# Summing over partitions with the values stationary: the sample attention's last reduction in a hybrid decoder layer

## The reference, cut to what matters

```
for window, d in DILATED_PATTERNS:              # (128,1), (512,4), (2048,16)
    s = einsum('bshe,bsnhe->bhsn', qf, kg) * scale + bias
    p = exp(s - m); den = sum(p)
    o = einsum('bhsn,bsnhe->bshe', p, vg) / den
return combine_patterns(outs, lses)             # weighted by the denominators
...
a.reshape(B, T, D_ATTN) * silu(ga)              # gate of the attention branch
```

## Time and profile before

| | |
|---|---|
| median of 3 executions | 902.86 us (902.83 to 903.67) |
| the profiled execution | 903.18 us |
| its span in the trace | 901.3 us |
| TensorE (PE) busy | 859.9 us, 95% |
| VectorE (DVE) busy | 565.9 us, 63% |
| ScalarE (ACT) busy | 402.5 us, 45% |
| GpSimd (POOL) busy | 52.1 us, 6% |
| instructions | 17338 |

### The profile page before, as it was taken

The page is one execution under the profiler, slowest core; times in us unless marked ns, Lnnn a source line. Parts: engine busy times, 40 slices in busy tenths (PEclk is TensorE's granted clock), DMA queues, the critical chain, the costliest instruction groups (busy, mean ns, idle before and its releaser), DMA issues. The chain is left out here.

```text
span 901.3 us, 17338 instructions
## 1 busy us (share of the span) xinstructions
PE 859.9 (95%) x7014; PEld 847.0 (94%) x7014; DVE 565.9 (63%) x1035; ACT 402.5 (45%) x896; POOL 52.1 (6%) x96
## 2 busy tenths in 40 slices
PE   7999999999999999999999999999989999999991
PEld 7999999999999999999999999999978999999990
DVE  5546866668676768667786767687779633333332
ACT  5745335524543453355246434533555433444333
POOL 3000000001000000100010000000000000000000
PEclk9999999999999999999999999999999999999996
DMA  8363455364526635553554266355565434434324
GB/s 300 113 166 99 122 149 146 93 161 133 142 83 149 174 91 134 140 148 93 141 158 129 86 155 174 87 131 150 150 167 155 127 107 120 124 109 124 110 59 189
DMA packets 207048, 121.36 MB, mean 135 GB/s; under 512 B 7576, under 2 KB 201760, under 8 KB 206432
## 3 DMA queue, kind: packets, MB, share of 16 engines
q1 hardware_dynamic: 202520, 111.20, 44.7%
q0 software_dynamic: 4448, 9.05, 3.1%
HBM read 108.04 MB, written 12.63 MB: 134 GB/s over the span
## 5 line engine op out<-in xcount | busy, mean ns | idle before, releaser
L547 PE MATMUL pj<-mov_hi,w_hi 128*128 128x260 f32 x2048 | 423.0, 288 | 0.5 <-DVE mov_lo L1425 0.5
L547 PE MATMUL pj<-mov_hi,w_lo 128*128 128x260 f32 x2048 | 412.0, 283 | 0.0
L547 PE MATMUL pj<-mov_lo,w_hi 128*128 128x260 f32 x2048 | 411.4, 282 | 0.0
L547 PEld LDWEIGHTS pj<-mov_hi,w_hi 128*128 128x128 f32 x2048 | 315.3, 189 | 2.1 <-DVE mov_lo L1425 0.7
L547 PEld LDWEIGHTS pj<-mov_lo,w_hi 128*128 128x128 f32 x2048 | 315.8, 188 | 0.0
L547 PEld LDWEIGHTS pj<-mov_hi,w_lo 128*128 128x128 f32 x2048 | 315.4, 188 | 0.0
L1103 DVE TENSOR_TENSOR w_lo<-w_raw,w_hi 128x640 fp32r<-128x640 f32 (+1 forms) x192 | 166.3, 866 | 213.5 <-ACT w_hi L745 212.6
L745 ACT ACTIVATE w_hi<-w_raw 128x640 fp32r<-128x640 f32 (+1 forms) x192 | 147.6, 769 | 187.2 <-PE pj L547 183.5
L801 ACT ACTIVATE pt_hi<-ps_t 128x128 fp32r<-128x128 f32 (+1 forms) x64 | 26.2, 436 | 78.9 <-PE ps_t L555 72.2
L1186 DVE TENSOR_TENSOR pt_lo<-ps_t,pt_hi 128x128 fp32r<-128x128 f32 (+1 forms) x64 | 29.6, 484 | 43.0 <-ACT pt_hi L801 43.0
L785 ACT ACTIVATE arena<-arena,stat 128x128 f32<-128x128 f32 (+1 forms) x64 | 35.5, 555 | 35.8 <-DVE stat L1172 35.8
(11 more groups left out here) (161 smaller groups left out, 710.3 us busy)
## 6 DMA issues: line engine op xcount, KB each, us to landing
w_raw<-in_w_in SPq DMA_DIRECT2D x96, 320.0 KB, 3.3
w_raw<-in_w_in SPq DMA_DIRECT2D x48, 384.0 KB, 3.6
arena<-in_cache_k_win SPq DMA_DIRECT2D x16, 384.0 KB, 5.4
arena<-in_cache_v_win SPq DMA_DIRECT2D x16, 384.0 KB, 8.1
w_raw<-in_w_out SPq DMA_DIRECT2D x16, 384.0 KB, 3.7
w_raw<-in_w_out SPq DMA_DIRECT2D x16, 320.0 KB, 3.0
arena<-row_scratch POOLq DMA_DIRECT2D x8, 512.0 KB, 5.0
arena<-in_cache_k_win SPq DMA_DIRECT2D x8, 512.0 KB, 6.4
```

The costliest lines, as they stand in the source:

```text
L547: mm = pe.matmul(pj[a][h][:, 0:HT], w, m[:, k, HT * h:HT * h + HT], start=(k == 0 and i == 0), stop=(c == 2 and k == KT - 1 and i == 2))
```

## The change

The operands of the sum over partitions change places. For each of the 8 samples the 128 x 128 block of `av_hi`, and then that of `av_lo`, is stationary, and two columns of ones are moving: 16 matmuls with 16 weight loads in place of four and four. The result for sample `b` lands as a column (and a copy of it beside it) in `ps_m`, one channel on each partition, so nothing is left to pick: one VectorE instruction multiplies every other column of the first 16 with the gate and writes `attn`. `ps_t` and `o_side` are no longer used, the semaphore `pick` goes, and its waiters wait for `mixed` or for `pool_mixed`.

```
-                elif pr > 0:
-                    pe.wait_ge(pick, 4 * pr)
+                elif pr >= 2 and pr % 2 == 0:
+                    pe.wait_ge(pool_mixed, pr)          # turn_p
...
                     if pr > 0:
-                        pe.wait_ge(pick, 4 * pr)
+                        pe.wait_ge(mixed, pr)           # step 10
...
-                    for b, dst in ((0, ps_m), (1, ps_t)):
-                        cols = slice(512 * b, 512 * b + 512)
-                        pe.matmul(dst[:, :], ones_r[:, :], av_hi[:, cols], start=True, stop=False)
-                        pe.matmul(dst[:, :], ones_r[:, :], av_lo[:, cols], start=False,
-                                  stop=True).then_inc(av_sum, 1)
+                    for b in range(NB):
+                        cols, to = slice(P * b, P * b + P), ps_m[:, 2 * b:2 * b + 2]
+                        pe.matmul(to, av_hi[:, cols], ones_r[:, 0:2], start=True, stop=False)
+                        mm = pe.matmul(to, av_lo[:, cols], ones_r[:, 0:2], start=False, stop=True)
+                    mm.then_inc(av_sum, 1)
...
-                    pe.wait_ge(pick, 4 * PAIRS)
+                    pe.wait_ge(mixed, PAIRS)            # turn_y(0)
...
-                if h == 0 and pr > 0:
-                    act.wait_ge(pick, 4 * pr)           # side
...
             def pick_rows(pr):
-                for b, src in ((0, ps_m), (1, ps_t)):
-                    dve.wait_ge(av_sum, 2 * pr + b + 1)
-                    if b == 1:
-                        dve.wait_ge(pick, 4 * pr + 2)
-                    else:
-                        dve.wait_ge(o_done, 2 * pr + 2)
-                    tmp = o_side.rearrange("p (b e) -> p b e", b=4)
-                    dve.tensor_tensor(tmp, src[:, :].rearrange("p (b e) -> p b e", b=4),
-                                      ident.unsqueeze(1).to_broadcast([P, 4, P]),
-                                      ALU.mult).then_inc(pick, 1)
-                    dve.wait_ge(pick, 4 * pr + 2 * b + 1)
-                    dve.tensor_reduce(attn[:, SEQ + 4 * b:SEQ + 4 * b + 4], tmp, AX_X,
-                                      ALU.add).then_inc(pick, 1)
-                dve.wait_ge(pick, 4 * pr + 4)
+                dve.wait_ge(av_sum, pr + 1)
                 dve.wait_ge(ga_gate, pr + 1)
-                dve.tensor_tensor(attn[:, SEQ:NT], attn[:, SEQ:NT], z_ga[:, SEQ:NT],
+                dve.tensor_tensor(attn[:, SEQ:NT], ps_m[:, 0:2 * NB:2], z_ga[:, SEQ:NT],
                                   ALU.mult).then_inc(mixed, 1)
```

More of the change, by code:

```diff
@@ L319, in layer_step @@
         av_sum = sem("av_sum")
-        pick = sem("pick")
         attn_gated, mixed = sem("attn_gated"), sem("mixed")
```

## The result

| | before | after |
|---|---|---|
| median of five executions | 903.06 us (902.83 to 904.52) | 913.2 us (911.25 to 914.98) |
| the profiled execution, its span | 903.18 us, 901.3 us | 914.98 us, 912.8 us |
| ratio of the times, 95% interval | | 1.0105 (1.009 to 1.0121) |

The kernel is slower by 10.1 us. The forecast of slower was right, the size was not: 909.2 us with a range up to 911.5. The profiled execution is the slowest of the five, so its account has to come out at more than the median's.

What follows compares the result with a forecast made beforehand. TensorE, busy 859.9 of 901.3 us, was taken to bound the kernel. Eight sums at 0.80 us, 6.4, less 0.13 made 6.3 us more: 909.2 us median, 907 to 911 at 0.75, 80% range 905.8 to 911.5.

Steps and rivals of the forecast that it cites:

- the sum 6.4 - 0.13: Whole kernel: 6.4 us added by eight sums' weight loads, less 0.13 us for a wait at block 15, giving 6.3 us.
- rival 3: Clock falls behind each pair's tiny matmuls, counted as a stand: 13.6 us more, 923; chance 0.03.
- The shift per sum: At each of eight sums, TensorE's next job starts 0.80 us later, 6.4 us in all.
- My formula: Delay of TensorE's next job behind each sum: 16 t - 0.96 us, t being the distance of two weight loads.
- the load and not the matmul sets the distance: At the scores behind a sum: weight loads take 0.11 us, 128-column matmuls 0.07 or less, so 16 loads take 1.76 us.
- the bounds of t: Distance of two weight loads in the sum: between 0.07 and 0.18 us, 1.3 to 15.4 us in all; 0.11 taken.
- VectorE is paced by TensorE: Throughout: VectorE waits on ScalarE, which waits for TensorE, so the delay reaches the end and 22 us less work buys idle time.
- rival 2: VectorE sets TensorE's pace and its relief shortens TensorE's waits: up to 8.4 us won, 900.8 us; chance 0.03.
- VectorE would wait some 1.4 us for the sum: At each pair's small instruction: VectorE waits some 1.4 us at no cost, done by 135.7 to 136.2, before 137.34.
- the wait at block 15: First output tile: TensorE's wait for the low part of block 15 goes, since `mixed` comes sooner: -0.13 us.
- in one place alone: In the steps following the sum's VectorE work, VectorE was said to idle 1.89 us at a single place.
- the shorter waits that the prediction had named as a sign against it: TensorE's waits for the bias and `av_lo` should keep 7.6 and 3.2 us; shrinking waits would show the prediction wrong.

Runs made afterwards that it cites:

- e5: The changed kernel with 128 columns of ones moving under the same 16 loads in place of two, results in two banks: 909.96 us, ratio 1.0074.
- e2: The changed kernel with 64 columns of ones moving under the same 16 loads in place of two: 911.15 us, ratio 1.0088.
- e10: The changed kernel run once more, unchanged, for a second profile: 912.65 us, ratio 1.0108 to the kernel before.
- e1: The kernel before with VectorE's half of the change alone; TensorE keeps its four wide matmuls, and attention values are wrong: 903.52 us, ratio 1.0001.
- e3: The changed kernel without the low part's eight matmuls, so eight weight loads a pair in place of 16: 903.33 us, ratio 0.9999.
- e6: The changed kernel with the sum queued on TensorE behind the same step's scores, not ahead of them: 908.23 us, ratio 1.0055.
- e7: The kernel before with its four-matmul sum queued on TensorE behind the same step's scores: 900.89 us, ratio 0.997.
- e9: The kernel before with the values moving as whole float32, unsplit, in two matmuls of 512 columns a pair: 902.91 us, ratio 0.9999.
- e8: The changed kernel with the values stationary as whole float32, unsplit, in eight matmuls of two columns: 904.58 us, ratio 1.0014.

## Why the prediction missed

**The account of the medians.** The kernels make a ladder: 903.3 us before (its median in the rounds of the experiments); 909.96 with 16 loads and no low clock behind a sum (e5), +6.6; 911.15 with the low clock behind the last sum (e2), +1.2; about 913 with falls behind some of the other seven as well (after, e10), +1.5 to 2. At 1.7 us a fall the last rung is one fall and not the two that both profiles show; but the profiled executions are 1.8 and 1.0 us above their medians, and the granted clocks of the nine (0.983 to 0.986, against 0.989 in e5) would be some two to three falls in all, an estimate from three digits. The forecast held the first rung: +6.3 predicted, +6.6 measured.

**The step that failed** is the clock: the sum 6.4 - 0.13 has no term for it behind the eight sums, and rival 3, which has it, got 0.03. The runs show 3.2 us in its place, 913.2 against the 909.96 of e5, which has the same loads and no low clock behind a sum, and three falls of 1.7 us each in both profiled executions. The rival was set out with its place and price, and the price of one fall was right (1.7 us). Two things in it were wrong. It took one stand in one execution as a rule: "after the 1.79 us stand at 652 it stayed at 1.00", and so a stretch of 0.5 + 1.8 us "nearer to the 1.79 that did nothing" was called safe. Six of twelve profiles have the low clock behind that very stand, among them e1 and the changed kernel itself, where two matmuls again take 0.43 us from 666.6 to 669.6. And it knew only all or nothing, 13.6 us for eight falls, where three of eight happened. Which sums are followed by a fall changes from one execution to the next: two profiles of one kernel have it behind different ones. A rival with "some of eight" would have stood at 911 to 914, inside what a range should hold.

The Trainium skill, in "TensorE: Matmul & The Clock Gate", Part 1, says that the gate's look at activity runs freely and does not start over with the kernel, and that the place of the rise at a kernel's start therefore varies from run to run. The two starts told above agree with it, full speed from 11.6 us or earlier in one and from 14.4 in the other, and the falls of the changed kernel's two profiles fit it (first, fourth, last against second, sixth, last).

**The term that was a little too small.** The shift per sum was given as 0.80 us and is 0.87, as the pairs of e2 and e5 show. Up to the first score it was right: from the first load of a sum to that matmul there are 1.81 us (135.26 to 137.07) in place of 1.02, 0.79 more. Two small errors cancel in this: the loads are 0.112 apart and not 0.110 (+0.03), and the matmul starts 0.02 to 0.03 us behind its load and not 0.06. The rest lies in the next job: before, the first score's load was done beneath a 512-column matmul, so the second score's load began with the first score's matmul, and the second matmul started 0.07 us after the first; in e2 they are 0.14 apart (135.88, 136.02), since every load there comes one behind the other. My formula stopped at the first score's start and did not follow the queue to where the two kernels run alike again. 8 x 0.07 = 0.6 us.

**Right by its own steps.** That the load and not the matmul sets the distance, read off the scores' loads; the bounds of t, 0.07 and 0.18, were not needed. The 81 ns a matmul that the Trainium skill gives in "TensorE: Matmul & The Clock Gate", section "Back-to-back issue gap", for pairs of a load and a matmul of 128 columns do not hold here: e5 has just such pairs, and they are 0.112 us apart. That VectorE is paced by TensorE and its relief is worth nothing (e1; rival 2 falls). That VectorE would wait some 1.4 us for the sum and end it all the same in time (1.44, and 0.17 us for the small instruction from the bank). That the wait at block 15 goes: in the traces of e1 and e5 every two matmuls there are 0.23 to 0.25 us apart and none 0.35, as before. Its 0.13 us is below what the medians can resolve.

**Slips that changed nothing.** The sum at 133.56 is the first pair's, made during the second pair's steps; the prediction calls it the second's. And VectorE idles not "in one place alone" behind it: the trace of before has 0.34 us at 139.86 and 0.88 us at 141.31 as well, which only adds to the idle time that the argument needs.

**In the last pair** the changed kernel's profile is 0.7 us shorter where 0.87 more was due. The low clock came there behind the stand of 1.79 us and not behind the one of 3.4, which shrank to 2.5: while TensorE is slow, VectorE goes on, so the fall is taken out of the next waits (1.3 us of them) and costs little. These are the shorter waits that the prediction had named as a sign against it; they are not VectorE's relief, since e3 and e6 have the relief and keep 7.6 and 2.2 us. e1 has this short form (69.35 us), e3 the long one (70.80), and both have before's median. What decides between the forms is open: six of the nine profiles with VectorE's relief have the short one, none of the three without it (before, e7, e9), which can still be chance. The 1.5 us between the forms also blur the rungs of the ladder, each a median of executions in either form.

**What stays open** is what exactly the gate asks for. The runs show a series in the length of the almost empty stretch, in the columns that move within it and in the stand ahead of it, with one or two profiles at each point; the times and mean clocks of four to eleven executions agree with them, but do not place the falls.

## What to carry to other kernels

Price a small matmul by its weight load: exchanging which operand is stationary turned 4 loads with 2048 columns beside them into 16 loads with 32, and 16 x 0.112 us is more than 0.99. When TensorE sets the time, the work saved on an engine that waits for it is worth nothing, even at 22 us.

A stretch in which TensorE does little but load weights can act on the clock like a stand, and here it added to the stand in front of it; moving 128 columns under the same loads cost nothing and kept the clock up. One execution without a low clock is no evidence that the stretch is safe: give such a fall a chance for each place, not one for all.

Look at what stands behind a wait in TensorE's own queue: putting the sum behind four short matmuls that were ready anyway gave 2.5 us.

## What the runs showed of the hardware that I had not expected

- A stretch of 1.8 us with 16 loads and 32 moving columns, behind a stand of 0.33 us in the profile, was followed by half the clock for about 3.4 us in three of eight places, and in three not all the same in a second profile; 3.6 us of it in all eight; 1.8 us without the stand in none of fifteen (e6, e8).
- A stand of 1.79 us between two chunks was followed by half the clock in six of twelve profiles.
- 64 or 128 columns moving under the loads left the loads at 0.112 us and, in the usual pairs, the clock at 1.00.
- A float32 matmul appears as two passes, each with its own load, 0.112 us apart with two columns moving; a pass of 512 columns took 0.43 us, float32r 0.23.
